# First two weight units of three stages multiplied ahead of the norm's root

## The reference

```
y  = x * rsqrt(mean(x*x) + eps) * g * (1 + scale) + shift     # norm and modulation, per token
out = y @ W                                                    # the stage's input projection
```

## Time and profile before

| | us |
|---|---|
| median of 3 runs (lowest, highest) | 2946.45 (2942.58, 2947.01) |
| the profiled execution, its own time | 2947.8 |
| its span, first to last instruction | 2946.0 |
| busy: TensorE / weight loads | 2838.8 / 2465.5 |
| busy: DVE / ACT / POOL | 1730.1 / 1452.4 / 1831.9 |
| moved by DMA | 621.49 MB, mean 211 GB/s |
| mean granted TensorE clock | 0.987 |

### The profile page before, as it was taken

The page is one execution under the profiler, slowest core; times in us unless marked ns, Lnnn a source line. Parts: engine busy times, 40 slices in busy tenths (PEclk is TensorE's granted clock), DMA queues, the critical chain, the costliest instruction groups (busy, mean ns, idle before and its releaser), DMA issues.

```text
span 2946.0 us, 48448 instructions
## 1 busy us (share of the span) xinstructions
PE 2838.8 (96%) x17785; PEld 2465.5 (84%) x17785; DVE 1730.1 (59%) x3151; ACT 1452.4 (49%) x2230; POOL 1831.9 (62%) x756
## 2 busy tenths in 40 slices
PE   6899999999899999999979999999999999999999
PEld 4788886777788898878869998999978888888888
DVE  5587895799776858548667886652334444442000
ACT  4222222566522532258647886755446555555443
POOL 1244443333254674445667777778878888888998
PEclk9999999999999999999989999999999999999999
DMA  9888621555665696233675554445556666665665
GB/s 405 347 322 316 263 98 58 196 194 210 231 237 201 247 368 264 79 129 115 226 302 170 166 169 144 151 151 178 174 183 210 233 236 229 233 214 195 204 205 185
DMA packets 147413, 621.49 MB, mean 211 GB/s; under 512 B 16288, under 2 KB 17616, under 8 KB 126288
## 3 DMA queue, kind: packets, MB, share of 16 engines
q1 hardware_dynamic: 146128, 614.48, 58.7%
q10 hardware_dynamic: 1152, 5.24, 0.5%
HBM read 617.54 MB, written 2.12 MB: 210 GB/s over the span
## 4 chain that ended last, share of the span: by engine, by line
issue 43%; PE 28%; POOL 27%; POOLq 1%; DVE 0%; ACT 0%; DVEq 0%; ACTq 0%
POOL w_low L695 27%; PE bank L739 18%; PE bank L747 9%; PE bank L730 1%; POOLq L690 0%; PE bank L731 0%; POOLq L694 0%; POOLq L695 0%; DVE bank L1775 0%; DVE bank L1780 0%; ACT region L1199 0%; PE bank L799 0%; DVE region L1823 0%; DVE h L1789 0%; DVE region L1826 0%
## 5 line engine op out<-in xcount | busy, mean ns | idle before, releaser
L695 POOL TENSOR_TENSOR w_low<-raw,w_high 128x1024 fp32r<-128x1024 f32 x752 | 1831.7, 2453 | 1103.4 <-ACT w_high L1199 1101.7
L1199 ACT ACTIVATE w_high<-raw 128x1024 fp32r<-128x1024 f32 x752 | 793.2, 1057 | 801.1 <-PE bank L747 611.0
L742 PE MATMUL bank<-h,w_high 128*128 128x256 f32 (+1 forms) x2816 | 889.5, 336 | 3.0 <-ACT region L1199 3.0
L743 PE MATMUL bank<-h,w_high 128*128 128x256 f32 (+1 forms) x2816 | 876.1, 332 | 0.0
L747 PE MATMUL bank<-h,w_low 128*128 128x256 f32 (+1 forms) x4416 | 754.9, 313 | 0.0
L747 PEld LDWEIGHTS bank<-h,w_low 128*128 128x128 f32 x4416 | 656.9, 190 | 65.5
L742 PEld LDWEIGHTS bank<-h,w_high 128*128 128x128 f32 x2816 | 535.6, 190 | 79.2 <-issue 19.0
L743 PEld LDWEIGHTS bank<-h,w_high 128*128 128x128 f32 x2816 | 535.6, 190 | 51.0 <-issue 1.0
L739 PE MATMUL bank<-h,w_high 128*128 128x512 f32 x1600 | 402.3, 393 | 3.6 <-ACT w_high L1199 3.6
L739 PEld LDWEIGHTS bank<-h,w_high 128*128 128x128 f32 x1600 | 288.7, 189 | 55.7 <-ACT w_high L1199 3.8
L1199 ACT ACTIVATE region<-bank 128x256 f32<-128x256 f32 (+3 forms) x313 | 140.1, 457 | 300.8 <-PE bank L747 271.4
(11 more groups left out here) (272 smaller groups left out, 3171.7 us busy)
## 6 DMA issues: line engine op xcount, KB each, us to landing
raw<-in_w_in SPq DMA_DIRECT2D x344, 512.0 KB, 3.8
raw<-in_w_up SPq DMA_DIRECT2D x176, 512.0 KB, 3.5
region<-in_w_rows SPq DMA_DIRECT2D x74, 1024.0 KB, 7.6
row_extra<-in_w_rows SPq DMA_DIRECT2D x54, 1024.0 KB, 7.0
raw<-in_w_out SPq DMA_DIRECT2D x96, 512.0 KB, 4.5
raw<-in_w_down SPq DMA_DIRECT2D x96, 512.0 KB, 3.4
row_extra<-in_w_half_rows SPq DMA_DIRECT2D x64, 512.0 KB, 4.2
region<-in_w_mods SPq DMA_DIRECT2D x23, 1024.0 KB, 11.2
```

What stands on the lines that cost most here:

```text
L695: nc.gpsimd.tensor_tensor(WL[s][:, part], RAW[s][:, part], WH[s][:, part], ALU.subtract) \
L742: nc.tensor.matmul(bank[:, 0:n], WH[slot][:, w], h, start=first and j == 0, stop=False)
L743: nc.tensor.matmul(bank[:, 0:n], WH[slot][:, w], l, start=False, stop=False)
L1199: return nc.scalar.activation(out, in_, func, **kw)
```

## The change

At three boundaries (called B1, B2 and B3 below: layer 0 to 1, first to second block, second block to the up projection) units 0 and 1 of the next stage are multiplied with x * gain instead of the normed tile. Its high and low part are made tile by tile in the out stage, and two columns are added to it, the high and low part of the shift. Behind the product, the root multiplies and the shift's column is added. Units 2 and 3 take the place of the pair that follows the norm. Four raw quarter loads lay a pair of units out so that slot 0 holds the first eight blocks of both.

TensorE (`second_pair` is the same loop for units 2 and 3, with the norm's tiles):

```diff
+        def early_pair(name, u, t0_, width):
+            for k in range(KT):
+                ready = max(k + 1, 1 if name != "in1" else 15 if k < 15 else KT)
+                pe.wait_ge(sem("n_hl"), H_AT[EARLY_AT[name]] + ready)
+                half = k // 8
+                for s in range(2):
...
+                    nc.tensor.matmul(L[s][:, 0:T + 2], WH[half][:, w], early_high(name, k, h_all), start=k == 0, stop=False)
+                    nc.tensor.matmul(L[s][:, 0:T], WH[half][:, w], early_low(name, k), start=False, stop=False)
+                    end = nc.tensor.matmul(L[s][:, 0:T + 2], WL[half][:, w], early_high(name, k, h_all), start=False, stop=k == KT - 1)
...
+                if k == 6:
+                    pe.wait_ge(sem("n_sums"), N_AT[name])
+                    nc.tensor.matmul(AUX[0][:, 0:width], ONES, NT_[:, 3, 0:width], start=True, stop=True) \
+                        .then_inc(sem("n_squsd"), 1)
```

ACT and DVE in the out stages:

```diff
+            def early(k):
...
+                act.wait_ge(sem("n_hl"), ready + k)
+                run(EARLY_BANK[name][:, lower], RES[:, k, :], ACT.Copy, scale=gain).then_inc(sem("n_tt"), 1)
+                run(early_high(name, k, lower), RES[:, k, :], ACT.Copy, scale=gain).then_inc(sem("n_hh"), 1)
+            def tile_done(k):
+                square(k // 4, k % 4)
+                early(k)
+            pair_rest(u0)
+            tile_done(0)
+            for k in range(2, KT):
+                ahead(u0 + k, k % 2, middle=lambda: tile_done(k - 1))
+            tile_done(15)
...
+        def done_before(name, n, k):
+            if k:
+                add_square(name, n, (k - 1) // 4, (k - 1) % 4)
+                early(name, k - 1)
```

(DVE's `early` is one subtraction of 256 columns. `middle` stands between the two highs of `ahead`.) ACT in layer 1's input stage:

```diff
-                act.wait_ge(sem("row_out"), ROW_DONE["out0"])
+                ahead(u, 0)
                 for n in range(KT):
-                    norm_high(H_AT["in1"], n, [(HH[:, n, upper], T_BANK["in1"][n % 4][:, lower], 48 + n, 0)])
+                    norm_high(H_AT["in1"], n, [(HH[:, n, upper], T_BANK["in1"][n % 3][:, lower], 48 + n, 0)])
+                    if n == 3:
+                        ahead(u + 1, 1)
+                        for m in range(2):
+                            early_shift(m)
+                            run(FIRST_OUT[:, m, :], L[m][:, 0:T], ACT.Copy).then_inc(bank_free[m], 1)
                     if n == 11:
-                        pair_first(u)
+                        ahead(u + 2, 0)
...
+                ahead(u + 3, 1)
+                act.wait_ge(sem("n_tt"), H_AT["ctx1"] + 4)
+                for n in range(2, 4):
+                    in_out(n)
+            for n in range(4 if l else 2, 20):
+                if l == 1 and n in (4, 8):
+                    act.wait_ge(sem("n_tt"), H_AT["ctx1"] + 2 * n)
                 if l == 1 and n == 12:
                     act.wait_ge(sem("n_hl"), H_AT["ctx1"] + KT)
                 ahead(u + n, n % 2, between=lambda: in_out(n))
-                if l == 1 and n < 10:
-                    for m in (2 * n - 4, 2 * n - 3):
+                if l == 1 and n < 12:
+                    for m in (2 * n - 8, 2 * n - 7):
                         norm_high(H_AT["ctx1"], m, [(HH[:, CTX[m], lower], T_CTX[m], 48 + CTX[m], 1)])
```

DVE there, and SP's rows:

```diff
                 inverse_root(upper, lower, 3)
+                dve.wait_ge(halves_done, 2 * U_IN[1] + 4)
                 for m in range(KT):
                     scaled([(T_CTX[m], CT0[:, CTX[m], :], gain0[:, CTX[m], 0:1], ROOT[:, upper])])
                 dve.wait_ge(sem("n_tt"), H_AT["ctx1"] + KT)
+                for b in range(2):
+                    dve.wait_ge(bank_free[b], 2 + T_IN[1] // 4)
+                seq(mul(uc[:, 0:2, :], FIRST_OUT, ROOT[:, lower].unsqueeze(1).broadcast_to([P, 2, T])))
                 rows_in1(0)
...
+                if e == 1:
+                    sp.wait_ge(halves_done, 2 * U_IN[1] + 4)
                 row_load("in1", e, dram["w_rows"][32 + e - 1])
...
                 sp.wait_ge(sem("at_y"), 12)
                 row_out1(1)
+                sp.wait_ge(sem("at_y"), 16)
                 row_out1(2)
```

SP's plan of rows between the units stays. In the second block's input stage ACT's loads of positions and others stand behind `ahead(U_IN2 + 3, 1)` and the outputs of units 2 and 3 (before: behind `pair_rest` and the outputs of units 0 and 1), and DVE takes one product and two additions for the first two outputs before it waits for the positions. In the up stage ACT now has this order:

```diff
-        pair_rest(U_UP)
-        for r in range(2):
-            up_half(0, r)
         for r in range(2):
             up_out(0, r)
         up_high(0, 0)
+        ahead(U_UP + 3, 1)
         for r in (2, 3):
-            ahead(U_UP + r, r % 2, between=lambda: up_half(0, r))
+            up_half(0, r)
+        for r in (2, 3):
             up_out(0, r)
         up_high(0, 1)
```

More of the change, by code:

```diff
@@ L566, in stream, with pair @@
             start = 0
+            def pair(i):
+                for half in range(2):
+                    for s in range(2):
+                        sp.wait_ge(split_ready, 2 * (u0 - 1) + 4 * i + 2 * half - 1 + s)
+                        sp.dma_start(RAW[half][:, HALF * s:HALF * (s + 1)], dram[name][first + 2 * i + s][:, HALF * half:HALF * (half + 1)]) \
+                            .then_inc(raw_in[half][s], 16)
             def two(i):
@@ L595, in stream @@
                 else:
-                    two(0)
-                    two(1)
+                    pair(0)
+                    pair(1)
                     evacuated(sp, T_OUT[0] + 16)
@@ L654, in stream @@
                         row_up((i - 3) // 2)
-                    two(i)
+                    if i < 2:
+                        pair(i)
+                    else:
+                        two(i)
                 return
+            if name == "w_in2":
+                for i in range(2):
+                    pair(i)
+                start = 2
             with sp.Fori(start, n // 2) as i:
@@ L1507, in _ @@
         act.wait_ge(sem("row_out"), ROW_DONE["in1"])
+        ahead(U_IN2, 0)
         for k in range(KT):
-            norm_high(H_AT["b1"], k, [(H2H[:, k, :], T_BANK["in1"][k % 4][:, lower], 96 + k, 2)])
+            norm_high(H_AT["b1"], k, [(H2H[:, k, :], T_BANK["in1"][k % 3][:, lower], 96 + k, 2)])
+            if k == 3:
+                ahead(U_IN2 + 1, 1)
+                for m in range(2):
+                    early_shift(m)
+                    run(U2[:, m, :], L[m][:, 0:T], ACT.Copy).then_inc(bank_free[m], 1)
             if k == 11:
-                pair_first(U_IN2)
+                ahead(U_IN2 + 2, 0)
         TURN = COEF[:, 4 * 64:5 * 64]
@@ L1598, in turned_p2 @@
             run(v["AT"][g % 2][:, 0:nk], BANK[6][:, 0:nk], ACT.Copy).then_inc(sem("a2_at"), 1)
-        pair_rest(U_IN2)
-        for n in range(2):
+        ahead(U_IN2 + 3, 1)
+        for n in range(2, 4):
             u_out(n)
@@ L1607, in _ @@
             act.dma_start(CST[n], dram["ssm_c"][n]).then_inc(sem(f"c_in{n}"), 16)
-        for n in range(1, 8):
-            if n > 1:
-                ahead(U_IN2 + n, n % 2, between=lambda: u_out(n))
+        for n in range(4, 8):
+            ahead(U_IN2 + n, n % 2, between=lambda: u_out(n))
             if n == 4:
@@ L1712, in up_out @@
             act.wait_ge(sem("up_sum"), n + 1)
[L1713 removed]
+            run(FT[:, r, :], (FIRST_UP[n] if isinstance(i, int) and n < 2 else L[r])[:, 0:T], ACT.Identity, bias=vec_at("conv_b", n),
                 scale=vec_at("conv_w", 3 * n + 2)).then_inc(sem("ffn_mid"), 1)
```

224 lines of the change are left out of this document (149 added, 75 removed).

## The result

| | before | changed |
|---|---|---|
| median (lowest, highest), us | 2946.73 (2942.58, 2948.55) | 2973.14 (2971.82, 2973.85) |
| profiled execution / its span, us | 2947.8 / 2946.0 | 2973.85 / 2972.1 |
| ratio, 95% interval | | 1.0092 (1.008 to 1.0104) |

What follows compares the result with a forecast made beforehand. TensorE was taken as the bound. B1 +25.7, B2 +2 and B3 0 sum to 27.7 us on the profiled 2947.8, giving 2975.5; the median, 1.35 lower, is 2974 us, range 2948 to 2992.

Steps and rivals of the forecast that it cites:

- B1: Into layer 1's input projection: boundary itself gains 6.4 us, but late loads behind it make the total +25.7 us.
- B2: Into the second block: +2 us (-3 to +8), including 1.5 us from layer 1's output stage.
- B3: Into the up projection: earlier boundary offset by unit 5 and 6 delays of 1.9 and 1.8 us; 0 us.
- 975.1: At B1: time in us at which the early pair, with the ones product, ends on TensorE.
- the 990.5: At B1: time in us at which units 2 and 3 end, against 996.9 before.
- The ring: Layer 1's input stage: unit 7's load waits for row 1, which waits for unit 6's weights; look-ahead shrinks from three units to one.
- a turn: One period of the ring: 9.0 plus 6.2, 15.2 us (13.3 to 18), where TensorE wants 5.76.
- The faster rival: Layer 1's input stage: units 6 and 7 land in time, so the ring does not close; 2942 us, 12%.
- row 2: Layer 1's output stage: its load moves behind the last head, adding 1.5 us (0 to 3.1).
- half clock behind it: At B2: TensorE's slow clock after the idle ahead of the scan, 2.5 us lost.
- The 14 us from landing to angle: At B2: VectorE's angle takes 14 us after the positions land, its last operations fast once GpSimd is idle; otherwise 18.8.

Runs made afterwards that it cites:

- e1: Changed kernel with ScalarE's context highs moved back two loop indices earlier, to their old lead: 2949.08 us, ratio 1.0009.
- e2: Changed kernel with SP's rows of layer 1's input stage each issued one unit later: 2946.99 us, ratio 1.0004.
- e3: Kernel before with only the change's late context highs on ScalarE, no early pair: 2968.62 us, ratio 1.008.
- e4: Changed kernel with context highs two indices earlier and SP's rows one unit later: 2942.42 us, ratio 0.9986.
- e5: e4 with the positions' load moved back behind the outputs of units 0 and 1, mid-norm: 2942.48 us.
- e9: Kernel before with row 2 of layer 1's output stage issued only behind the last head: 2947.38 us, ratio 1.0005.
- e6: e4 with the rotary angle's intermediate results in a PSUM bank instead of SBUF: 2938.41 us, ratio 0.9977.
- e10: e4 plus angle results in PSUM and layer 1's last output-stage unit loaded ahead of the last row: 2937.15 us, ratio 0.9973.

## Why the prediction held, point by point

- **Boundary B1.** Early pair without a gap, ones product inside it, slower norm tiles behind: -6.4 forecast, -5.6 measured. The pauses at tiles 4 and 12 were put at 1.3 and 1.8 us; the rows show 0.41 and 2.01. (The 1.3 is a slip: 975.1 + 4 x 0.72 = 978.0, and tile 4 at 979.6 is 1.6 late, which is the figure that the 990.5 and the step for B3 use.)
- **The ring.** Forecast: row 0 ends at 1000.6, a turn takes 15.2, units 6, 7, 8, 10 and 12 are late, nothing behind unit 14. Measured: 1002.6 (2 of it the offset), turns of 15.3, 15.4 and 14.9, the same five units, and the lateness of 28.1 constant from unit 14 on. The two halves of the turn, 9.0 and 6.2, came out as 9.0 (1008.88 to 1017.9) and 6.9 (1017.95 to 1024.82), and in the next turn as 8.5 and 6.3. Unit 14 starts at 1082.55 where the forecast, with the offset added, has 1082.5. e1, e2 and e3 show that it is this ring. That B1 came out to the tenth (25.7) is partly luck all the same: the forecast's own bounds for a turn, 13.3 to 18, gave 18 to 37. From unit 4 to the end of the stage the loss is 28.1 + 3.3 = 31.4 us. 22.3 are waits, and 6.5 go with the half clock behind the three long ones: the first halves of units 6, 7 and 8 take 4.96, 5.28 and 4.93 us where 2.88 is the pace (granted clock 0.88 over the 115 us, where the earlier trace rows have 1.00). The prediction took unit starts from ScalarE's highs, so both were in its turn; but it had waits of 5 to 8 us for units 6, 7, 8 and 10, and they were 4.50, 7.96, 6.36 and 1.07.
- **The faster rival** had as its point that unit 7's load is issued by 1006 rather than 1015; it was issued at 1018.32. In e4, where unit 7 is issued at 1003.32, the rival's time (2942) is what was measured.
- **B2.** The sum was right to 1.3 us, and that is luck: its steps were wrong by more and cancel. Forecast were +1.5 (row 2), -1.7 (up to the scan) and +2.5 (half clock behind it); measured were +3.4, -5.5 and +2.8. First, "the positions' load is moved behind units 2 and 3" was taken as what the angle waits for; e5 shows that the landing is hidden, and two additions that I had put at nothing hold VectorE for 4.41 us. The angle began 6.0 us behind the end of unit 3 instead of 4.3, and took 11.5 us instead of 14. Second, row 2's later load was given 1.5 us; it costs nothing (e9), while the last unit's wait did grow by 3.0, from a cause that is open. Third, the early pair was to stand before the ones product and did not, one reason why the four units took 38.9 and not 41.2. The wait ahead of the scan (5 forecast) was 3.85.
- **The shared port.** The 14 us from landing to angle rested on single operations being slow only while GpSimd runs. In the changed kernel they take 2.40 at 1598.24 and 0.29 at 1603.09, and in e6, with one side in PSUM, 0.43. By the rule of the Trainium skill, "SBUF — State Buffer", section "Who interferes with whom", the pair of ports that the two engines share is an exclusive lock; the trace agrees (2.40 against 0.29), and e6 shows how to step around it.
- **B3.** Boundary -4.2 forecast, -5.2 measured; highs late by 1.9 and 1.8, together 3.7 of loss forecast, 4.0 measured (2.0 each). The chain of the first up tiles took 5.7 us (2248.33 to 2254.01; forecast 5.8). The forecast's start of unit 5's highs, 2227.9, does not follow from its own terms (2221 + 5.8 = 2226.8); the rows have 2226.7 with the 27.3 taken off. So the 1.9 came out right in part by luck.
- **Not forecast**: 1.5 us that a wait behind layer 1's input stage got shorter (4.38 to 2.60), and the 2.3 us of offset at the start; together 0.8.

## What to carry to other kernels

When a step is moved later in one engine's order, follow its result round: if another engine's queue puts the load of unit k + 6 behind something that now needs unit k + 5, the look-ahead of the whole pipeline is gone, whatever each engine's busy share. Count how many units the loop spans before and after, take its length from the rows, and compare that with the span times TensorE's pace; here 15.2 us against one unit of 5.76 gave the loss to within a microsecond, closer than its own bounds allowed to expect. The ring was cut here at two of its engines, ScalarE and SP, and the cheaper cut was one constant in SP's plan.

## What the runs showed of the hardware

- Operations of VectorE on 256 columns with both sides in SBUF took 2.2 to 2.4 us while GpSimd ran and 0.29 when it was idle; with one side in PSUM they took 0.42 to 0.49 with GpSimd running throughout (e6). A slow chain of eight went from 11.5 to 3.7 us.
- An idle time of TensorE of the same length does not always cost the same: behind the 2.20 us ahead of the ones product after the scan, the granted clock stayed full in e4 and e10 and fell to 0.93 over the next 25 us in e6 (1.5 us). In the ring, the first products behind waits of 4.50, 7.96 and 6.36 us took 0.58 us, and 0.38 and 0.39 behind waits of 1.07 and 2.40; but in e3 the one behind a wait of 2.25 took 0.58 as well (granted clock 0.51 in the 3 us from 1063).
